# Encoder trunk on one core: where the low halves of the split operands, three squares and an activation table are handled around the norms

## The reference, cut to what matters

```
def _rmsnorm(x, g):
    y = xf * lax.rsqrt(jnp.mean(xf * xf, axis=-1, keepdims=True) + EPS)
    return (y * g.astype(jnp.float32)).astype(x.dtype)

def _swiglu(h, w_gu, w_down):
    g, u = jnp.split(h @ w_gu, 2, axis=-1)
    return (jax.nn.silu(g) * u) @ w_down

    for i in range(DEPTH):
        h = _rmsnorm(x, norm_mix_g[i])
        x = x + _mlstm_mixer(...)        # or _gla_mixer(...)
        h = _rmsnorm(x, norm_ffn_g[i])
        x = x + _swiglu(h, ffn_w_gu[i], ffn_w_down[i])
    return _rmsnorm(x, norm_final_g)
```

## Time and profile before

| | |
|---|---|
| time, median of 3 runs (lowest, highest) | 1786.25 us (1784.65, 1787.35) |
| the profiled execution: its time, its span | 1784.6 us, 1782.7 us |
| busy: TensorE, VectorE, ScalarE, GpSimd | 1743.8 (98%), 1069.9 (60%), 672.5 (38%), 229.5 (13%) us |
| mean granted TensorE clock | 0.995 |
| the chain that ended last | TensorE 91%, VectorE 5%, ScalarE 2% |

### The profile page before, as it was taken

The page is one execution under the profiler, slowest core; times in us unless marked ns, Lnnn a source line. Parts: engine busy times, 40 slices in busy tenths (PEclk is TensorE's granted clock), DMA queues, the critical chain, the costliest instruction groups (busy, mean ns, idle before and its releaser), DMA issues.

```text
span 1782.7 us, 26143 instructions
## 1 busy us (share of the span) xinstructions
PE 1743.8 (98%) x10234; PEld 1704.9 (96%) x10234; DVE 1069.9 (60%) x1846; ACT 672.5 (38%) x1166; POOL 229.5 (13%) x253
## 2 busy tenths in 40 slices
PE   7999999998999999999999999999999999999998
PEld 6999888998999999999989999999999999999998
DVE  6141454359767585858561357632886776767675
ACT  5222455243424242424342346741533333333233
POOL 4000121450000000000230024335200000000002
PEclk9999999999999999999999999999999999999999
DMA  5320001502122212121232100141021212121212
GB/s 176 110 71 25 25 24 48 169 13 87 49 71 72 71 60 83 60 83 60 83 119 71 48 25 24 47 143 54 19 95 61 82 48 95 48 86 45 83 60 83
DMA packets 108929, 123.60 MB, mean 69 GB/s; under 512 B 4721, under 2 KB 105137, under 8 KB 108561
## 3 DMA queue, kind: packets, MB, share of 16 engines
q1 hardware_dynamic: 107760, 122.00, 20.7%
q10 hardware_dynamic: 1056, 0.07, 0.0%
HBM read 112.62 MB, written 9.44 MB: 68 GB/s over the span
## 4 chain that ended last, share of the span: by engine, by line
PE 91%; DVE 5%; ACT 2%; issue 1%; DMA 1%; POOL 0%; SPq 0%; DVEq 0%; POOLq 0%; ACTq 0%
PE bank L436 90%; DVE xT L1815 1%; DVE qkv L1797 1%; DVE w_lo L1614 1%; DVE w_lo L1647 1%; ACT w_hi L1070 0%; DMA raw<-in_mlstm_w_out_dram 0%; DVE w_lo L1620 0%; POOL h_lo L2349 0%; DMA xs<-in_x_prompt_dram 0%; ACT w_hi L1077 0%; PE bank L1058 0%; PE bank L697 0%; DVE y_fin L2243 0%; PE bank L546 0%
## 5 line engine op out<-in xcount | busy, mean ns | idle before, releaser
L436 PE MATMUL bank<-y_parts,w_hi 128*128 128x384 f32 x2560 | 660.1, 339 | 11.5 <-DVE rstd L1684 7.1
L436 PEld LDWEIGHTS bank<-y_parts,w_hi 128*128 128x128 f32 x2560 | 465.0, 189 | 14.6 <-issue 9.0
L436 PE MATMUL bank<-h_hi,w_hi 128*128 128x384 f32 x1280 | 438.8, 343 | 4.1 <-DVE w_lo L1620 1.8
L436 PE MATMUL bank<-h_lo,w_hi 128*128 128x384 f32 x1280 | 432.8, 338 | 0.0
L436 PE MATMUL bank<-y_parts,w_lo 128*128 128x384 f32 x1280 | 432.4, 338 | 0.0
L436 PE MATMUL bank<-h_hi,w_lo 128*128 128x384 f32 x1280 | 432.3, 338 | 0.0
L436 PEld LDWEIGHTS bank<-h_hi,w_hi 128*128 128x128 f32 x1280 | 240.8, 188 | 13.5 <-POOL h_lo L2349 3.5
L436 PEld LDWEIGHTS bank<-h_lo,w_hi 128*128 128x128 f32 x1280 | 240.9, 188 | 1.2 <-issue 0.2
L436 PEld LDWEIGHTS bank<-h_hi,w_lo 128*128 128x128 f32 x1280 | 240.9, 188 | 0.6
L436 PEld LDWEIGHTS bank<-y_parts,w_lo 128*128 128x128 f32 x1280 | 241.3, 189 | 0.0
L1815 DVE TENSOR_TENSOR xT<-xT,bank 128x384 f32<-128x384 f32 x224 | 123.6, 552 | 188.4 <-PE bank L436 182.4
(11 more groups left out here) (228 smaller groups left out, 2126.7 us busy)
## 6 DMA issues: line engine op xcount, KB each, us to landing
raw<-in_ffn_w_gu_dram SPq DMA_DIRECT2D x44, 1024.0 KB, 5.0
raw<-in_ffn_w_down_dram SPq DMA_DIRECT2D x40, 512.0 KB, 3.4
raw<-in_gla_w_in_dram SPq DMA_DIRECT2D x12, 1024.0 KB, 5.4
raw<-in_mlstm_w_in_dram SPq DMA_DIRECT2D x11, 1024.0 KB, 5.3
x_keep<-xT SPq DMA_DIRECT2D x2, 3072.0 KB, 9.6
xT<-x_keep SPq DMA_DIRECT2D x8, 768.0 KB, 6.7
raw<-in_mlstm_w_out_dram SPq DMA_DIRECT2D x4, 1024.0 KB, 7.0
raw<-in_gla_w_out_dram SPq DMA_DIRECT2D x4, 1024.0 KB, 6.2
```

Of the source, the lines that this page charges most:

```text
L436: return nc.tensor.matmul(out, lhsT, rhs, start=start, stop=stop)
```

## The change

There are four edits.

- The low parts of T4 and T3 leave VectorE. GpSimd makes them, T4 first, in block 0 of each layer, behind its squares and ahead of the memsets; TensorE waits for T3 and T4 on a new semaphore, `t_low_pool`. VectorE's T1 low part stands one unit earlier.
- At norms 1 to 3, GpSimd adds the squares only up to n = 12. n = 13, 14 and 15 are added by VectorE (`last_square`); at the odd norms ScalarE now squares 13 and 14 too, ahead of Ln.
- `norm` loads no table.
- The low parts of the first half of norms 1 to 3 go from GpSimd to VectorE (`norm_both`), interleaved with the scaling.

```diff
-GROUP_SQ = (0, 0, 1, 15, 16)
+GROUP_SQ = (0, 0, 3, 17, 20)
...
                 if L is not None:
-                    pe.wait_ge(t_lo, 4 * L + 2)
+                    pe.wait_ge(t_low_pool, 2 * L + 2)
                 pe.wait_ge(op_lo, 6 * u + 3)
                 product(2, 2, *t_parts(3)).then_inc(p_done, 1)
...
             def norm(e, q):
 
-                log_exp_table()
+                if e % 2:
+                    squares(q - 2, e, (13, 14))
                 norm_rstd(e, 0)
                 norm_high(e, 0, range(4))
                 squares(q - 2, e, (15,))
...
                 a_low(f, 2, 1, 0, 0)
-                t_low(L, 3, 2)
                 times(3)
...
-            def norm_second(e):
+            def norm_both(e, half, k0, k1):
 
                 def low(c):
-                    s = NORM_S[e] + KC + c
+                    s = NORM_S[e] + KC * half + c
                     dve.wait_ge(hi_ready, s + 1)
-                    dve.wait_ge(lo_ready, s)
-                    src = h_chunk(c, 1) if e % 2 else ht[:, s % 4, :]
-                    V.tensor_tensor(h_lo[:, c, halves[1]], src, h_hi[:, c, halves[1]].bitcast(F32), ALU.subtract
-                                    ).then_inc(lo_ready, 1)
-
-                for c in range(KC):
-                    norm_half(e, 1, (c,))
+                    src = h_chunk(c, half) if e % 2 else ht[:, s % 4, :]
+                    V.tensor_tensor(h_lo[:, c, halves[half]], src, h_hi[:, c, halves[half]].bitcast(F32),
+                                    ALU.subtract).then_inc(lo_ready, 1)
+
+                for c in range(k0, k1):
+                    norm_half(e, half, (c,))
                     if c:
                         low(c - 1)
-                low(KC - 1)
+                if k1 == KC:
+                    low(KC - 1)
+
+            def last_square(e, n):
+
+                dve.wait_ge(group_sq, GROUP_SQ[e] + (n - 12 if e % 2 else n - 1))
+                dve.wait_ge(sq_acc, 16 * (e - 1) + n)
+                V.tensor_tensor(sq_sum[:, n // 14, :], sq_sum[:, n // 14, :], sg[:, n % 4, :], ALU.add
+                                ).then_inc(sq_acc, 1)
...
                                     ALU.subtract).then_inc(w_lo_ready, 1)
+                    last_square(e, 13)
                     add_residual(q, 1, 2, c + 2)
-                    norm_half(e, 0, range(4))
+                    norm_both(e, 0, 0, 3)
                     add_residual(q, 1, 3, c + 3)
-                    norm_half(e, 0, range(4, KC))
-                    dve.wait_ge(group_sq, GROUP_SQ[e + 1])
-                    dve.wait_ge(sq_acc, 16 * e - 1)
-                    V.tensor_tensor(sq_sum[:, 1, :], sq_sum[:, 1, :], sg[:, 3, :], ALU.add).then_inc(sq_acc, 1)
+                    norm_both(e, 0, 3, 6)
+                    last_square(e, 14)
+                    last_square(e, 15)
+                    norm_both(e, 0, 6, KC)
                     split(q + 1, 1)
                     if e == 2:
                         gates_taken(1, 0)
-                    norm_second(e)
+                    norm_both(e, 1, 0, KC)
...
                             fast_low(q + 1, 0, fast, j)
-                            if first == 1 and j == 4:
+                            if first and j == 3:
                                 t_low(L, 1, 4)
-                    if first == 4:
-                        t_low(L, 4, 3)
...
             def squares(q, e):
 
-                for n in range(15):
+                for n in range(13 if e < 4 else 15):
...
-                if e < 4:
-                    norm_low(e, 0)
...
                 for b, nb in enumerate(BLOCKS):
+                    if b == 0:
+                        for n, i in ((4, 3), (3, 2)):
+                            pool.wait_ge(t_hi, 4 * L + i)
+                            hi, lo = [p.rearrange("p (h c) t -> p h c t", h=2) for p in t_parts(n)]
+                            G.tensor_tensor(lo, t_source(n), hi.bitcast(F32), ALU.subtract).then_inc(t_low_pool, 1)
                     if L == 0 and b == 0:
 
                         G.memset(g_hi[:, :, :].bitcast(mybir.dt.uint32), 0)
```

More of the change, by code:

```diff
@@ L313, in build @@
         p_copied, c_read, s_act, at_done = sem("p_copied"), sem("c_read"), sem("s_act"), sem("at_done")
-        group_sq, t_sum, t_hi, t_lo = sem("group_sq"), sem("t_sum"), sem("t_hi"), sem("t_lo")
+        t_low_pool, group_sq, t_sum, t_hi, t_lo = sem("t_low_pool"), sem("group_sq"), sem("t_sum"), sem("t_hi"), sem("t_lo")
         fin_copied = [sem(f"fin_copied{i}") for i in range(2)]
@@ L513, in fast_tile @@
                 if L is not None:
-                    pe.wait_ge(t_lo, 4 * L + 1)
+                    pe.wait_ge(t_lo, 2 * L + 1)
                 pe.wait_ge(op_lo, 6 * u + 2)
@@ L523, in fast_tile @@
                 if L is not None:
-                    pe.wait_ge(t_lo, 4 * L + 4)
+                    pe.wait_ge(t_lo, 2 * L + 2)
                 pe.wait_ge(op_lo, 6 * u + 5)
@@ L2305, in _ @@
                         V.tensor_tensor(w, w_a2_raw[32:64, :, :], w.bitcast(F32), ALU.subtract).then_inc(a2_split, 1)
-                    pair(q0 + PDN[b], 0, nb=nb, first=None if b else 4)
+                    pair(q0 + PDN[b], 0, nb=nb)
                     if b + 1 < len(BLOCKS):
```

## The result

The changed kernel takes 1790.15 us (median of 10 runs, 1788.59 to 1792.07), the kernel before 1785.95 us on the same chip (10 runs, 1784.3 to 1787.35). The ratio is 1.0026, 95% interval [1.0016, 1.0035]: slower, by 4.2 us where 7.75 were forecast. The profiled execution of the changed kernel took 1789.35 us.

What follows compares the result with a forecast made beforehand. TensorE was taken to bound the kernel. Terms -3.2 + 0.4 + 9.7 + 0.95 = +7.85 us took the profiled execution from 1784.6 to 1792.4; 1.65 more for the median gave 1794.0 us, range 1790.5 to 1798.5 (8 in 10).

Steps and rivals of the forecast that it cites:

- TensorE is the bound and a new wait adds in full: Whole kernel: TensorE is busy 1743.8 of 1782.7 us, so only 39 us can be gained and new waits add in full.
- with the stall TensorE's tile ends last: Layer 0, block 0: behind the new wait TensorE's tile ends at 438.9 us, and VectorE's sums start at 439.6, not 429.90.
- Norm 2, -3.2 us: At norm 2 TensorE starts the first low part 1.82 us earlier and the clock stays up, giving 1.4 us more.
- Norms 1 and 3, +0.4 us: At norms 1 and 3 the next weight tile's low part ends at 389.3 against 389.09 us: +0.2 us each.
- Layer 0, +9.7 us: Layer 0, block 0: memsets behind GpSimd's low parts delay the gate cast; TensorE waits 9.6 us for `w_lo`, sum +9.7 us.
- its price of 4.0 us for 128x1536: Each T3 or T4 subtraction on GpSimd, taken from two of 384 elements in 2.00 us; bounds 3.4 and 5.0 us.
- Its low clock, put at 1.4 to 1.7 us: Layer 0, block 0: the clock falls behind TensorE's 9.6 us wait, costing another 1.4 to 1.7 us.
- the whole sum would be 1.2 us less: Total over the kernel if each GpSimd subtraction takes 3.4 us, by the skill's measured ratio of 1.96.
- rival C: Smaller stall in layer 0: GpSimd at 3.4 us, clock kept or weights the only bound; +5.4, 1791.6 us; chance 0.13.
- the T4 slot removed from VectorE: Layer 0: the 1.75 us of T4's low part leaving VectorE is no gain, since TensorE's tile ends last.
- Layer 1, +0.95 us: Layer 1, block 0: GpSimd's subtractions hold VectorE's `w_lo` twice, so the sums and all behind come 0.95 us later.
- The wait of about 0.9 us: Layer 1: a TensorE wait of about 0.9 us expected in the profile ahead of the first seven-product tile.

Runs made afterwards that it cites:

- the T low parts alone: The kernel before with only T3's and T4's low parts moved to GpSimd ahead of the memsets, T1's one unit earlier, norms untouched: 1791.88 us, ratio 1.0035.
- The load alone: The kernel before without the table load at the three norms, nothing else changed: 1784.03 us, ratio 0.9994.
- the memsets first: The changed kernel with GpSimd's three memsets ahead of T4's and T3's low parts in block 0 of layer 0: 1785.34 us, ratio 1.0005.
- the pieces: The changed kernel with GpSimd's memsets ahead of T4's and T3's low parts, each subtraction cut in four of 128x384: 1780.64 us, ratio 0.9980.

## Why the prediction was right, and where its sizes were off

The kernel got slower, at the place and by the chain that the prediction names. The size was off, and the time came out just below the stated range.

- **TensorE is the bound and a new wait adds in full.** Right: the stall of 8.61 us with its low clock is 9.0 us of span. The wait and the 1.9 us of low clock make 10.5. But before the change the sums of the seven-product tile began at 429.90, 2.4 us after TensorE had ended its down tile (423.3 + 24 x 0.175 = 427.5). Now they begin at 439.11, 0.8 us after it (438.3). The prediction has this step: with the stall TensorE's tile ends last.
- **Norm 2, -3.2 us.** Right, in part by luck: -3.24. TensorE waits 0.51 and 1.00 us where 0.89 and 2.42 stood; that is 1.8 us and repeats in every kernel with these edits. The other 1.4 are the fall of the clock that is gone. It was there in both executions of the kernel before, but not with the T low parts alone, where the wait is 2.44 us. The load alone gives 0.6 of the 3.2.
- **Norms 1 and 3, +0.4 us.** The stretches up to them changed by under 0.1 us each. But the bound was drawn on the low part alone. TensorE now comes 1 us earlier and waits 1.8 us there instead of 0.76. No time is lost by the wait itself, yet it brings the clock into play: behind the 1.8 us it fell in one of the two places, 1.56 us. The prediction did not see that a wait can grow at no cost and then cost by the clock.
- **Layer 0, +9.7 us.** The mechanism was right at every step: GpSimd's order, the gate cast, `g_lo`, the residual adds, `w_lo`, TensorE. The term was mis-sized, 9.02 measured, since its price of 4.0 us for 128x1536 is 3.5. Its low clock, put at 1.4 to 1.7 us, cost TensorE 1.9. The Trainium skill, GPSIMD Engine Reference, section 3.1, with its ratio of 1.96 had given an estimate of 3.4; here it is 3.5/1.75 = 2.0. The nearest rows of the trace, 384 elements alone or beside VectorE, were the worse guide. The prediction also says that at 3.4 us the whole sum would be 1.2 us less. By its own terms it is 2.45 less, 1.2 in layer 0 and 1.25 in layer 1, as in rival C. That the T4 slot removed from VectorE would be no gain behind the stall held: it showed only in the kernels without a stall, with 0.8 us in layer 0.
- **Layer 1, +0.95 us.** This is the step that failed in sign: -0.38. VectorE is held twice, as forecast (2.26 and 1.56 us for 0.69), but with 3.5 us for the first and 3.96 for the second both end before TensorE is kept waiting. The wait of about 0.9 us that the prediction looked for is not there: TensorE waits 3.57 us for `rstd`, as before. The working had given -0.3 for 3.4 us; it was the same mis-sized price. The hold itself is a little shorter than the prediction reads from the earlier trace rows: `w_lo` took 0.65 us longer there while GpSimd worked on for 0.78, so not exactly as much.
- **What the lock does, and where.** The prediction looked for it in layer 1 only, since in layer 0 VectorE stood idle. With the memsets first layer 0 is 1.95 us slower than in the kernel before (from norm 1 to the seven-product tile 58.02 and 56.07 us, both without low clock), and 2.7 slower than with the pieces, because the held instruction is `g_lo`, with four residual adds and `w_lo` queued behind it. The Trainium skill, SBUF — State Buffer, "SBUF: two separate sides", has the shared pair going to one engine for a whole instruction: the rows of the memsets-first kernel and of the pieces agree, 3.68 against 1.16 us for the same `g_lo`.
- **The sum.** With 9.02, -0.38 and nothing at norms 1 and 3 the terms give -3.24 + 9.02 - 0.38 = +5.4 us, the figure of rival C. The profiled execution showed +4.7, which the falls of the clock elsewhere and the rest of the ledger make up (-1.36 + 1.56 + 1.10 - 0.18 - 1.82 = -0.7), and the medians +4.2. These falls nearly cancel, which is chance. Rival C with its 1791.6 us was nearer than the forecast, by its price of 3.4 us; that the clock would be kept, which it also names, did not come true. The range gave nothing for the clock's chance, and its lower end stood on C without it.

## What to carry to other kernels

Before work is put on an idle engine, read what already stands behind it in that engine's list: here three memsets, done 30 us ahead of need, were pushed to the far side of 7 us of work, and that cost more than the rest of the change gave. Where GpSimd and VectorE both read SBUF, cut GpSimd's work into short instructions: it worked 1.8 us longer in layer 0, and the kernel was some 4.6 us faster, 3.1 of them seen in the rows. A cast and its low part in sequence on two engines are worth halving where TensorE waits for the second; here each of the two places gave 0.8 us of wait.
